# Attention in a two-layer hybrid decoder step: how far ahead of its use a unit's scores and sigmoid are made

## The chip, the cores and the metric

The kernel runs on one core of a Trainium2 chip. The metric is the device time of one execution of the whole program in microseconds (us), lower is better. Engines are named as the profile names them: PE is TensorE (matmuls and transposes; PEld are its weight loads), DVE is VectorE, ACT is ScalarE, POOL is GpSimd, SP is SyncE. Each engine works through its own instructions in the order in which they were written, and the engines hand work to each other through semaphores.

## The reference

Two layers (`DEPTH = 2`), each on a prompt of 1024 rows and on 8 sample sequences of 8 rows with a paged past of 4096. A layer projects the normed input into three token mixers side by side: retention (6 heads), stick-breaking attention (5 heads, "sb") and forgetting attention (5 heads, "fox"); their gated outputs are joined, projected, and a per-layer embedding is added. All is float32. What matters here are the two attentions on the prompt:

```python
# stick-breaking, a block of 128 query rows pb
z = einsum('bthd,bshd->bhts', qb, k) * scale
mask = k_pos < pb
ln1m = where(mask, log_sigmoid(-z), 0)
excl = reverse cumulative sum of ln1m, without the own element
a = where(mask, exp(log_sigmoid(z) + excl), 0)
out = einsum('bhts,bshd->bthd', a, v)

# forgetting
s = einsum(...) * scale + c_query - c_key
p = softmax(where(k_pos <= pb, s, -inf))
out = einsum('bhts,bshd->bthd', p, v)
```

## The kernel before, in words

A layer goes through phases that all engines leave together: projections and retention, then sb attention on the prompt (`ATT_S`), sb decoding of the samples, projections, fox attention on the prompt (`ATT_F`), fox decoding, output projections. The change lies in the two attention phases. With two layers each runs twice, so there are four such stages in the program.

An attention stage is a list of 40 **units**, `UNITS` at L466: 8 blocks of 128 query rows, the longest first (`t` from 7 down to 0, `i = 7 - t`), and in each block 5 heads (`h` from 0 to 4). A unit has `n = (t + 1) * 128` keys: 1024 in the first block, 128 in the last. I call the five units of a block a row of units, by its n. The steps of a unit u, with the engine and the line:

- **scores** (PE, L946): queries times keys into PSUM banks 0 and 1 or 2 and 3, by the parity of u.
- For sb: **sigmoid** (ACT, `first`, L1404) from PSUM into `sig[:, u % 2]`. Then **stick** (DVE, L1856, L1857, L1860, L1864): mask the diagonal block, take one minus it, scan the product backwards, multiply. It writes `att[:, u % 2]` and counts `att_probs`.
- For fox: **largest** (DVE, L1872 and L1875): mask the diagonal block in PSUM and take the row maximum. Then **exp** (ACT, `first`, L1413) from PSUM into `expd[:, u % 2]` with the sum of the row.
- **turn** (PE, L958): `t + 1` transposes of the weights into PSUM banks 4 and 5, which have no second copy. It waits for the stick (sb) or the exp (fox) of u and for the copy of unit u-1.
- **copy** of the turned weights (ACT, `to_sbuf`, L1424) to one of three SBUF buffers.
- **weigh** (PE, L972): turned weights times values. It is issued for a pair of heads after h = 1 and h = 3 and for the last head alone after h = 4.
- Once a row of units: **copy out** (ACT, `copy_out`, L1431 and L1432), **back** (PE, L984, three transposes), **finish** (DVE, L1887; in fox also L1884 and L1886), which gates the result into `O`. They belong to the row before and are issued while the next row is under way: copy out after h = 1, back at h = 2, finish after h = 3.

Nothing plans the order: it is the order in which the loops are written out. On PE the turn of u stands behind the scores of u+1, the weigh of u-1 and, at h = 2, the back. On ACT the copy of u stands behind the sigmoid or exp of u+1. On DVE it is stick or largest by unit, with finish behind the unit with h = 3.

Two waits bound how far ahead a step can go: scores of u wait until the sigmoid or exp of u-2 has read the PSUM banks (`att_first`, L943), and the sigmoid of u waits until the stick of u-2 is through with `sig` (`att_probs`, L1403). The exp of u waits for the turn of u-2.

Of the kernel before, what the change touches and what calls it, by code (L numbers as in the profile page):

```python
# [214 lines left out]
def step_program(nc, x_prompt, x_sample, state_ret, cache_sb_k, cache_sb_v, cache_fox_k,  # L215
# [10 lines left out]
    with ExitStack() as ctx:  # L226
# [220 lines left out]
        def phase_over(eng, n):  # L447

            eng.drain().then_inc(phase_sem, 1)  # L449
            eng.wait_ge(phase_sem, 4 * (n + 1))  # L450
# [15 lines left out]
        UNITS = [(t, NT - 1 - t, h) for t in reversed(range(NT)) for h in range(HA)]  # L466
# [9 lines left out]
        def weighed(u):  # L476

            t, i, h = UNITS[u]
            return QP * i + h // 2 + 1
# [6 lines left out]
        def bank2(first, n=1024):  # L486
            return ps[:, first:first + 2, :].rearrange("p b c -> p (b c)")[:, 0:n]
# [266 lines left out]
        def _(pe):  # L754
# [177 lines left out]
            def attention(phase):  # L932
                kind = KIND[phase]
                qT, kT, v = (qT_s, kT_s, v_s) if kind == "sb" else (qT_f, kT_f, v_f)

                def scores(u):
                    t, i, h = UNITS[u]
                    n = (t + 1) * P
                    q = slice((h % 2) * HD, (h % 2) * HD + HD) if kind == "sb" else slice(0, HD + 1)
                    a = h // 2 if kind == "sb" else h  # L940
                    if u >= 2:

                        pe.wait_ge(att_first[kind], u - 1)  # L943
                    for c in range(0, n, 512):
                        w = min(512, n - c)
                        ins = pe.matmul(ps[:, 2 * (u % 2) + c // 512, 0:w], qT[q, a, t * P:(t + 1) * P],  # L946
                                        kT[q, a, c:c + w], start=True, stop=True)
                    ins.then_inc(att_scores[kind], 1)

                def turn(u):  # L950
                    t, i, h = UNITS[u]

                    pe.wait_ge(att_probs[kind] if kind == "sb" else att_first[kind], u + 1)
                    if u >= 1:
                        pe.wait_ge(attT_ready[kind], u)
                    src = att if kind == "sb" else expd
                    for j in range(t + 1):
                        ins = pe.transpose(ps[:, 4 + j // 4, (j % 4) * P:(j % 4 + 1) * P],  # L958
                                           src[:, u % 2, j * P:(j + 1) * P], ident)
                    ins.then_inc(att_turned[kind], 1)  # L960

                def weigh(u):

                    t, i, h = UNITS[u]
                    pe.wait_ge(attT_ready[kind], u + 1)
                    c = h // 2
                    if c == 0 and i >= 2:
                        pe.wait_ge(att_done[kind], i - 1)
                    heads = [(a, 2 * c + a) for a in range(2) if 2 * c + a < HA]
                    for j in range(t + 1):  # L970
                        for a, hh in heads:
                            ins = pe.matmul(ps[a * HD:(a + 1) * HD, 6 + t % 2, c * P:(c + 1) * P],  # L972
                                            v[:, j, hh * HD:(hh + 1) * HD],
                                            attT[kind][(u - h + hh) % 3][:, j * P:(j + 1) * P],
                                            start=(j == 0), stop=(j == t), tile_position=(0, a * HD),
                                            skip_group_check=True)
                    ins.then_inc(att_out[kind], 1)

                def back(t):

                    pe.wait_ge(att_copied[kind], NT - t)
                    for c in range(QP):
                        w = min(P, DA - c * P)
                        ins = pe.transpose(ps[:, 6 + t % 2, c * P:c * P + w], att_oT[kind][0:w, c * P:(c + 1) * P],  # L984
                                           ident[0:w, 0:w])
                    ins.then_inc(att_back[kind], 1)

                scores(0)
                for u, (t, i, h) in enumerate(UNITS):
                    if u + 1 < len(UNITS):  # L990
                        scores(u + 1)
                    if u >= 1 and UNITS[u - 1][2] in (1, 3, 4):
                        weigh(u - 1)
                    if h == 2 and i >= 1:
                        back(t + 1)
                    turn(u)
                weigh(len(UNITS) - 1)
                back(0)
                phase_over(pe, phase)
# [203 lines left out]
            with pe.Fori(0, DEPTH) as L:  # L1203
# [5 lines left out]
                project(PROJ_SEGS[PROJ_S], L)  # L1209
                phase_over(pe, PROJ_S)  # L1210
                attention(ATT_S)
                decode(DEC_S, L)
                project(PROJ_SEGS[PROJ_F], L)
                phase_over(pe, PROJ_F)
                attention(ATT_F)
                decode(DEC_F, L)
                turn_mixed(0)
# [19 lines left out]
        def _(act):  # L1237
# [155 lines left out]
            def attention(phase):  # L1393
                kind = KIND[phase]

                def first(u):
                    t, i, h = UNITS[u]
                    n = (t + 1) * P
                    if kind == "sb":
                        act.wait_ge(att_scores[kind], u + 1)  # L1400
                        if u >= 2:

                            act.wait_ge(att_probs[kind], u - 1)  # L1403
                        act.activation(sig[:, u % 2, 0:n], bank2(2 * (u % 2), n), ACT.Sigmoid)\  # L1404
                            .then_inc(att_first[kind], 1)
                    else:
                        act.wait_ge(att_max, u + 1)
                        if u >= 2:
                            act.wait_ge(att_turned[kind], u - 1)

                        if h == 0 and i >= 2:
                            act.wait_ge(att_done[kind], i - 1)
                        act.activation(expd[:, u % 2, 0:n], bank2(2 * (u % 2), n), ACT.Exp,  # L1413
                                       bias=small[:, 40 + u % 4:41 + u % 4],
                                       accum_out=small[:, 50 + (t % 2) * HA + h:51 + (t % 2) * HA + h])\
                            .then_inc(att_first[kind], 1)

                def to_sbuf(u):
                    t, i, h = UNITS[u]
                    act.wait_ge(att_turned[kind], u + 1)  # L1420
                    if u >= 3:
                        act.wait_ge(att_out[kind], weighed(u - 3))
                    n = (t + 1) * P
                    act.activation(attT[kind][u % 3][:, 0:n], bank2(4, n), ACT.Copy).then_inc(attT_ready[kind], 1)  # L1424

                def copy_out(t):

                    act.wait_ge(att_out[kind], QP * (NT - t))
                    if t < NT - 1:
                        act.wait_ge(att_back[kind], NT - 1 - t)  # L1430
                    act.activation(att_oT[kind][:, 0:2 * P], ps[:, 6 + t % 2, 0:2 * P], ACT.Copy)  # L1431
                    act.activation(att_oT[kind][0:HD, 2 * P:3 * P], ps[0:HD, 6 + t % 2, 2 * P:3 * P], ACT.Copy)\  # L1432
                        .then_inc(att_copied[kind], 1)

                first(0)
                for u, (t, i, h) in enumerate(UNITS):
                    if u + 1 < len(UNITS):
                        first(u + 1)
                    to_sbuf(u)
                    if h == 1 and i >= 1:  # L1440
                        copy_out(t + 1)
                copy_out(0)
                phase_over(act, phase)
# [707 lines left out]
```

## Time and profile before

| | us |
|---|---|
| median of 3 runs | 3688.18 |
| the 3 runs | 3682.5, 3688.18, 3698.48 |
| the profiled execution | 3678.38 |
| its span | 3676.8 |
| sb attention, layer 1 and layer 2 | about 460 to 598, 2288 to 2424 of the span |
| fox attention, layer 1 and layer 2 | about 1092 to 1224, 2915 to 3047 |

Over the span PE is busy 3204.2 us (87%), DVE 1365.4 (37%), ACT 950.5 (26%). The profile is one execution; a group of its instructions is named by line, engine, operation and output and input. "Idle before, releaser" is how long an engine stood still before an instruction and whose semaphore ended it. The granted clock (PEclk) is 1.00 when PE runs at 2.4 GHz and 0.50 at 1.2 GHz. Instructions of the same kind that follow each other are merged in a timeline, with their count behind an x; the duration of a merged PE row contains the tail of its last matmul, so the next row can start up to 0.2 us before it ends. A float32 score matmul of 512 columns shows as two records.

### The profile page before, as it was taken

How to read it: one execution, taken by the hardware profiler on the slowest of the kernel's cores; microseconds unless marked ns; L12 is line 12 of the kernel's file. 1: busy time of each engine (PE TensorE's matmuls, PEld its weight loads, DVE VectorE, ACT ScalarE, POOL GpSimd, SP SyncE). 2: the span in 40 equal slices, each digit the busy share in tenths (PEclk: the TensorE clock that was granted, in tenths of full speed). 3: DMA queues.
4: the chain of work that ended last, by engine and by line, in shares of the span. 5: the costliest groups of instructions: out<-in, count | busy, mean ns of one | idle time of the engine just before them, and what ended most of it. 6: DMA issues, size and time to landing. Idle time of an engine off the chain costs nothing. (4 is left out here: it accounts for less than half of the span.)

```text
span 3676.8 us, 67694 instructions
## 1 busy us (share of the span) xinstructions
PE 3204.2 (87%) x25256; PEld 1989.8 (54%) x25256; DVE 1365.4 (37%) x3002; ACT 950.5 (26%) x1746; POOL 597.8 (16%) x1090
## 2 busy tenths in 40 slices
PE   6999987888998688799989998978889987887998
PEld 4556654555666455444455666545556654554443
DVE  3235086443224444312142350954433244442211
ACT  2012144332224333211020122433322242331110
POOL 0000000444010044400000000004440101452000
PEclk9999988999999799899989999989999997998999
DMA  5011103887120388710120011048861205995102
GB/s 175 18 36 33 50 10 105 265 287 244 38 83 1 117 278 290 249 66 16 46 96 28 28 45 44 1 129 288 284 217 33 72 1 173 295 299 186 57 29 72
DMA packets 268657, 439.67 MB, mean 120 GB/s; under 512 B 48818, under 2 KB 216403, under 8 KB 268339
## 3 DMA queue, kind: packets, MB, share of 16 engines
q1 hardware_dynamic: 205810, 239.96, 20.4%
q0 software_dynamic: 55744, 189.25, 15.6%
q10 hardware_dynamic: 6912, 7.87, 0.6%
q8 instruction: 126, 2.06, 0.2%
q14 instruction: 65, 0.52, 0.0%
HBM read 410.28 MB, written 26.65 MB: 119 GB/s over the span
## 5 line engine op out<-in xcount | busy, mean ns | idle before, releaser
L806 PE MATMUL ps<-W,xT 128*128 128x320 f32 (+7 forms) x5120 | 1482.9, 465 | 11.5 <-DVEq L449 11.5
L806 PEld LDWEIGHTS ps<-W,xT 128*128 128x128 f32 (+1 forms) x5120 | 856.7, 184 | 585.6 <-issue 291.5
L688 POOL DMA_DIRECT2D branch<-in_cache_sb_v_dram x480 | 258.8, 539 | 637.5 <-issue 597.3
L688 POOL DMA_DIRECT2D branch<-in_cache_fox_v_dram x480 | 258.9, 539 | 621.2 <-issue 579.6
L1468 ACT ACTIVATE branch<-ps 128x512 f32<-128x512 f32 x288 | 165.6, 595 | 386.6 <-PE ps L1051 378.2
L1051 PE MATMUL ps<-C,W 128*128 128x128 f32 x1280 | 199.4, 301 | 73.1 <-DMA W<-in_cache_fox_k_dram 26.6
L1051 PE MATMUL ps<-C,branch 128*128 128x128 f32 x1280 | 194.9, 295 | 65.7 <-DMA branch<-in_cache_sb_k_dram 18.0
L1136 PE MATMUL ps<-branch 128*8 128x64 f32 x9920 | 182.2, 234 | 55.9 <-DMA branch<-in_cache_fox_v_dram 27.6
L1073 PE MATMUL ps<-branch,work 128*32 128x512 f32 x896 | 229.9, 631 | 0.8 <-issue 0.2
L1051 PEld LDWEIGHTS ps<-C,W 128*128 128x128 f32 x1280 | 151.0, 151 | 141.0 <-issue 67.4
L1051 PEld LDWEIGHTS ps<-C,branch 128*128 128x128 f32 x1280 | 147.8, 149 | 146.3 <-issue 96.1
L946 PE MATMUL ps<-branch 64*128 64x512 f32 (+7 forms) x480 | 209.4, 564 | 19.9 <-POOLq L449 19.9
L1136 PEld LDWEIGHTS ps<-branch 128*8 128x8 f32 x9920 | 158.8, 99 | 79.7 <-issue 33.9
L1980 DVE COPY branch<-ps 128x512 f32<-128x512 f32 x160 | 107.8, 688 | 199.8 <-PE ps L1051 199.6
L1476 ACT ACTIVATE work<-ps 128x512 f32<-128x512 f32 x160 | 92.2, 597 | 317.5 <-PE ps L1073 317.5
L652 POOL DMA_DIRECT2D out_dram<-work x32 | 17.7, 552 | 742.9 <-ACT work L1292 549.0
L1073 PE MATMUL ps<-W,work 128*32 128x512 f32 x384 | 136.0, 657 | 1.6 <-issue 1.6
L946 PEld LDWEIGHTS ps<-branch 64*128 64x128 f32 (+1 forms) x480 | 85.7, 210 | 81.3 <-issue 59.9
L1995 DVE COPY branch<-ps 128x64 f32<-128x64 f32 x256 | 46.3, 226 | 211.7 <-PE ps L1087 160.8
L1087 PE MATMUL ps<-C,work 128*128 128x128 f32 x640 | 102.6, 293 | 24.2 <-ACT work L1476 24.2
L1692 DVE TENSOR_TENSOR work<-ps,branch 128x512 f32<-128x512 f32 (+1 forms) x40 | 25.5, 638 | 251.0 <-PE ps L806 250.6
L1860 DVE TENSOR_TENSOR_SCAN branch<-branch 128x1024 f32<-128x1024 f32 (+7 forms) x80 | 108.7, 1358 | 2.7
(246 smaller groups left out, 3389.1 us busy)
## 6 DMA issues: line engine op xcount, KB each, us to landing
branch<-in_cache_sb_v_dram POOLq DMA_DIRECT2D x480, 160.0 KB, 4.3
branch<-in_cache_fox_v_dram POOLq DMA_DIRECT2D x480, 160.0 KB, 4.1
W<-in_cache_sb_k_dram SPq DMA_DIRECT2D x248, 160.0 KB, 3.4
W<-in_cache_fox_k_dram SPq DMA_DIRECT2D x248, 160.0 KB
branch<-in_cache_sb_k_dram SPq DMA_DIRECT2D x240, 160.0 KB, 4.2
branch<-in_cache_fox_k_dram SPq DMA_DIRECT2D x240, 160.0 KB, 4.3
W<-in_w_in_dram SPq DMA_DIRECT2D x14, 1280.0 KB, 6.3
W<-in_w_in_dram SPq DMA_DIRECT2D x9, 1536.0 KB, 7.1
```

The costliest lines, as they stand in the source:

```text
L688: pool.dma_start(ringV[:, g % 2, p * DA:(p + 1) * DA], cache[L, bass.ds(pg, 1)].rearrange("a s h d -> s (a h d)"))\
L806: ins = pe.matmul(out, src[:, k, t * P:t * P + R], W[i % 2][:, k, a:z], start=(k == 0), stop=(k == kc - 1), **place)
L946: ins = pe.matmul(ps[:, 2 * (u % 2) + c // 512, 0:w], qT[q, a, t * P:(t + 1) * P], kT[q, a, c:c + w], start=True, stop=True)
L1051: ins = pe.transpose(ps[:, n % 2, m * P:(m + 1) * P], ringK[g % 2][:, at:at + P], ident)
L1073: ins = pe.matmul(ps[q:q + 32, bank, :], q_now[:, kk, :], kT_d[(5 * g + kk) % SLOTS], start=True, stop=True, tile_position=(0, q), skip_gr ...
L1087: ins = pe.transpose(ps[:, 6 + j % 2, m * P:(m + 1) * P], z_rows[:, 2 if j == 4 else j % 2, m * P:(m + 1) * P], ident)
L1136: ins = pe.matmul(out(h, a), pr[:, h, :, g * PG8 + first + p], values[:, c:c + HD], start=False, stop=False, tile_position=(0, 32 * a), sk ...
L1468: act.activation(kT_d[n % SLOTS], ps[:, n % 2, :], ACT.Copy).then_inc(s["kt_act"], 1)
L1476: act.activation(z_rows[:, 2 if j == 4 else j % 2, :], ps[:, 3 if j == 4 else (5 if j % 2 else 2), :], ACT.Copy)\
L1860: link(dve.tensor_tensor_scan(prod[:, e:SEQ][:, ::-1], r[:, ::-1], r[:, ::-1], 1.0, ALU.mult, ALU.bypass))
L1980: dve.tensor_copy(kT_d[n % SLOTS], ps[:, n % 2, :]).then_inc(s["kt_dve"], 1)
L1995: dve.tensor_copy(by_pair[:, j, 2 * NEW * kk:2 * NEW * (kk + 1), :, 0], src[:, kk, 0:2 * NEW])
```

## The change

On PE the scores of the first two units are made ahead of the loop, and the loop then makes those of u+2 where it made those of u+1. On ACT, in the sb stages alone, the sigmoids of the first two units stand ahead of the loop, and the loop makes that of u+2 ahead of the copy of u. In the fox stages ACT keeps its order (`ahead = 1`), and DVE keeps its order in both. No semaphore, buffer, instruction or operand is added or removed; the waits inside each step are the same.

```diff
                 scores(0)
+                scores(1)
                 for u, (t, i, h) in enumerate(UNITS):
-                    if u + 1 < len(UNITS):
-                        scores(u + 1)
+                    if u + 2 < len(UNITS):
+                        scores(u + 2)
                     if u >= 1 and UNITS[u - 1][2] in (1, 3, 4):
                         weigh(u - 1)
                     if h == 2 and i >= 1:
...
                 first(0)
+                ahead = 2 if kind == "sb" else 1
+                if ahead == 2:
+                    first(1)
                 for u, (t, i, h) in enumerate(UNITS):
-                    if u + 1 < len(UNITS):
-                        first(u + 1)
+                    if u + ahead < len(UNITS):
+                        first(u + ahead)
                     to_sbuf(u)
                     if h == 1 and i >= 1:
                         copy_out(t + 1)
```

ACT, the first units of an sb stage, before (L1404 is the sigmoid, L1424 the copy of turned weights; semaphores that a row waits for stand in brackets):

```order
L1404 ACTIVATE branch<-ps 128x1024 [waits phase_sem]
L1404 ACTIVATE branch<-ps 128x1024 [waits att_scores_sb]
L1424 ACTIVATE work<-ps 128x1024 [waits att_turned_sb]
L1404 ACTIVATE branch<-ps 128x1024 [waits att_probs_sb,att_scores_sb]
L1424 ACTIVATE work<-ps 128x1024 [waits att_turned_sb]
```

And the same place after the change (the lines are numbered one higher there):

```order
L1405 ACTIVATE branch<-ps 128x1024 [waits phase_sem]
L1405 ACTIVATE branch<-ps 128x1024 [waits att_scores_sb]
L1405 ACTIVATE branch<-ps 128x1024 [waits att_probs_sb,att_scores_sb]
L1425 ACTIVATE work<-ps 128x1024 [waits att_turned_sb]
L1405 ACTIVATE branch<-ps 128x1024 [waits att_probs_sb,att_scores_sb]
```

The third sigmoid now stands ahead of the first copy, and so on down the stage: each sigmoid is one copy earlier.

PE, in a fox stage, from the back of the first row of units on (L984 back, L958 turn, L946 scores, L972 weigh), before:

```order
L984 MATMUL ps<-C,branch 128x64
L958 MATMUL ps<-C,work 128x128 [waits attT_ready_fox,att_first_fox]
L958 MATMUL ps<-C,work 128x128 x6
L946 MATMUL ps<-branch 128x512 [waits att_first_fox]
L946 MATMUL ps<-branch 128x384
L958 MATMUL ps<-C,work 128x128 [waits attT_ready_fox,att_first_fox]
L958 MATMUL ps<-C,work 128x128 x6
L946 MATMUL ps<-branch 128x512 [waits att_first_fox]
L946 MATMUL ps<-branch 128x256
L972 MATMUL ps<-work,branch 64x128 [waits attT_ready_fox]
```

And after:

```order
L984 MATMUL ps<-C,branch 128x64
L958 MATMUL ps<-C,work 128x128 [waits attT_ready_fox,att_first_fox]
L958 MATMUL ps<-C,work 128x128 x6
L946 MATMUL ps<-branch 128x512 [waits att_first_fox]
L946 MATMUL ps<-branch 128x256
L958 MATMUL ps<-C,work 128x128 [waits attT_ready_fox,att_first_fox]
L958 MATMUL ps<-C,work 128x128 x6
L946 MATMUL ps<-branch 128x512 [waits att_first_fox]
L946 MATMUL ps<-branch 128x256
L972 MATMUL ps<-work,branch 64x128 [waits attT_ready_fox]
```

The pattern of steps stays; what moved is which unit the scores belong to. Behind the back stood the scores of the last unit of this row (896 keys, 512 and 384); now the scores of the first unit of the next row stand there (768 keys, 512 and 256), and those of the last unit are already ahead of the back.

## Rows read from the trace of the kernel before

**Rows 1.** Stretches: us, busy us (instructions) of PE, PEld, DVE, ACT, POOL, PEclk

```profile
463.00:594.00 131.00, 111.73 (x674) 68.25 (x670) 115.23 (x167) 55.76 (x94) 0.00 (x0) 0.89 0.00 1
1097.00:1220.00 123.00, 103.52 (x674) 68.86 (x672) 53.31 (x110) 60.20 (x134) 0.00 (x0) 0.90 0.01 3
```

**Rows 2.** Waits of DVE, sb stages of layers 1 and 2: total us, times, longest

```profile
DVE branch L1856 <- ACT branch L1404: 14.1, 10, 5.8
...
DVE branch L1856 <- ACT branch L1404: 12.7, 8, 6.2
```

**Rows 3.** The same view, last row of units of the sb stage, layer 1

```profile
DVE branch L1856 <- ACT branch L1404: 1.8, 3, 0.8
```

**Rows 4.** Timeline of DVE, sb layer 1: where sticks 0, 4 and 5 start

```profile
466.12 0.29 DVE L1856 TENSOR_TENSOR branch<-branch,C 128x128 f32<-128x128 f32 x1 [5.82 <-ACT branch L1404]
...
490.36 0.29 DVE L1856 TENSOR_TENSOR branch<-branch,C 128x128 f32<-128x128 f32 x1 [2.60 <-ACT branch L1404]
...
494.88 0.28 DVE L1856 TENSOR_TENSOR branch<-branch,C 128x128 f32<-128x128 f32 x1
```

**Rows 5.** Timeline of ACT, same stage: the sigmoid of unit 4

```profile
489.30 1.03 ACT L1404 ACTIVATE branch<-ps 128x1024 f32<-128x1024 f32 x1 [0.89 <-PE ps L946]
```

**Rows 6.** Stretches of that stage where the clock rises and where it is low again

```profile
484.00:488.00 4.00, 4.00 (x26) 3.26 (x23) 3.69 (x3) 0.61 (x1) 0.00 (x0) 0.63 0.00 0
...
588.00:592.00 4.00, 4.00 (x15) 2.33 (x15) 2.88 (x10) 1.72 (x7) 0.00 (x0) 0.50 0.00 0
```

**Rows 7.** Waits of PE for the copy, fox stages of layers 1 and 2

```profile
PE ps L972 <- ACT work L1424: 11.9, 12, 1.4
PE ps L972 <- ACT branch L1424: 6.1, 5, 1.5
...
PE ps L972 <- ACT work L1424: 11.7, 12, 1.4
PE ps L972 <- ACT branch L1424: 5.9, 5, 1.4
```

**Rows 8.** The same view, last row of units of the fox stage, layer 1

```profile
PE ps L972 <- ACT branch L1424: 1.5, 1, 1.5
PE ps L972 <- ACT work L1424: 1.2, 3, 0.6
```

**Rows 9.** Timeline of PE, fox layer 1, row of units of 640 keys

```profile
1172.67 0.76 PE L958 MATMUL ps<-C,work 128*128 128x128 f32 x5
1173.27 1.25 PE L946 MATMUL ps<-branch 65*128 65x512 f32 x4
1174.36 0.71 PE L958 MATMUL ps<-C,work 128*128 128x128 f32 x5
1174.90 1.02 PE L946 MATMUL ps<-branch 65*128 65x512 f32 x2
```

**Rows 10.** Timeline of ACT and DVE at the same place

```profile
1173.47 0.70 ACT L1424 ACTIVATE branch<-ps 128x640 f32<-128x640 f32 x1 [1.47 <-PE ps L958]
...
1173.53 0.49 DVE L1887 TENSOR_TENSOR O<-O,ps 128x320 f32<-128x320 f32 x1
1174.56 0.30 DVE L1872 TENSOR_TENSOR ps<-ps,C 128x128 f32<-128x128 f32 x1 [0.54 <-PE ps L946]
1174.89 0.82 DVE L1875 TENSOR_REDUCE small<-ps 128x1 f32<-128x640 f32 x1
...
1175.75 0.79 ACT L1413 ACTIVATE work<-ps,small 128x640 f32<-128x640 f32 x1 [1.57 <-DVE small L1875]
```

**Rows 11.** Duration of the maximum and the exp over all shapes: ns min/median/max

```profile
L1875 DVE TENSOR_REDUCE small<-ps x80: 291/758/1226, 1096.4 to 3038.8; 128x1 f32<-128x1024 f32 x10, 128x1 f32<-128x896 f32 x10, 128x1 f32<-128x768 f32 x10, 128x1 f32<-128x640 f32 x10
...
L1413 ACT ACTIVATE work<-ps,small x80: 359/740/1117, 1099.0 to 3039.2; 128x1024 f32<-128x1024 f32 x10, 128x896 f32<-128x896 f32 x10, 128x768 f32<-128x768 f32 x10, 128x640 f32<-128x640 f32 x10
```

**Rows 12.** Stretches of the fox stages with the clock below full, layers 1 and 2

```profile
1116.00:1148.00 32.00, 27.99 (x184) 20.43 (x183) 12.09 (x22) 14.20 (x23) 0.00 (x0) 0.84 0.00 1
...
2940.00:2948.00 8.00, 6.96 (x52) 5.61 (x53) 1.85 (x3) 3.11 (x5) 0.00 (x0) 0.79 0.01 2
```

## The prediction

> **What bounds the kernel now.** I read the page first: 40 units run in each of four attention stages, some 540 us of the span of 3676.8 (the table of stages). Nothing outside these stages is touched, so a gain can only come from what engines stand still in them. Next came the busy time of the two kinds of stage: in sb DVE is busy 115.2 of 131 us and PE 111.7; in fox PE is busy 103.5 of 123 us, and DVE and ACT 53 and 60 [rows 1]. So sb goes by DVE and fox by PE, and the question is who makes that engine wait. The view of waits answers it. In sb DVE waits for the sigmoid (L1404), 14.1 us in layer 1 and 12.7 in layer 2, of which 5.8 and 6.2 are the very first one [rows 2]. In fox PE waits in front of the weigh for the copy (L1424), 18.0 and 17.6 us in 17 waits each [rows 7]. The timeline then shows what the awaited instruction itself had waited for.
>
> **sb, what moves.** Before, the scores of u+1 stood on PE in front of the turn of u, and on ACT the sigmoid of u+2 stood behind the copy of u, which needs that turn. Now both are one unit earlier. The sigmoid of u+2 needs only its scores and the end of the stick of u, and DVE is by then busy with the stick of u+1, so the sigmoid lies beside a whole stick. The copy gives way by one sigmoid (1.03 us at 1024 keys [rows 5]); it is waited for by the weigh, behind scores on an engine with slack. Nothing is issued more often, there is no DMA among the steps, and SP's and POOL's queues are not passed.
>
> The waits that can go are 14.1 - 5.8 = 8.3 and 12.7 - 6.2 = 6.5, 14.8 us [rows 2]; the first wait stays, since scores and sigmoid of unit 0 come as before. Two deductions. In the last row of units DVE waits 1.8 us [rows 3] while PE is busy all the time at the lower clock [rows 6], so there PE sets the pace and an earlier place in the order gives little: I take off 1.8 for each layer and give back 0.3 for each, for the gap before the last turn. And in the first row PE runs at the lower clock until late in the stretch of [rows 6], about 487. A stick of 1024 keys takes 494.88 - 490.36 = 4.52 us; four of them from 466.12 end at 484.2 and the fifth at 488.7, while sticks 4 and 5 began at 490.36 and 494.88 [rows 4]. If the clock rises no earlier, PE makes the scores of unit 5 where it made those of unit 4, just ahead of the sigmoid at 489.30 [rows 5], and stick 5 begins where stick 4 did, at 490.36: 4.5 us gained and 1.6 left as a wait. If PE, which now has the scores of unit 2 to do in its pause ahead of the first turn, gets its clock earlier, none is left. Between 0 and 1.6 in layer 1, and less in layer 2, whose waits are smaller, I take 0.9 together. sb: 14.8 - 3.6 + 0.6 - 0.9 = 10.9 us.
>
> **fox, what goes.** ACT's order is exp of u+1, then copy of u. Before, where no weigh stood between (after h = 1 and h = 3), PE ran scores of u+1, turn of u, scores of u+2, and then the weigh of u waited: the copy was behind the exp of u+1, that behind the maximum, and that behind scores just made. Now those scores were made a unit earlier, the exp of u+1 can run while PE turns u, and the copy is ready when the weigh comes. That takes away the 35.6 us [rows 7] except in the last row of units, where no scores are left to fill with and 2.7 us stay in each layer [rows 8]: 35.6 - 5.4 = 30.2.
>
> **fox, what comes.** The scores of u+2 now wait for the exp of u, one step closer than before. DVE keeps its order, and there the finish of the row before stands ahead of the maximum of the unit with h = 4. Before, that was covered, since DVE was through with the finish and still waited 0.54 us for scores [rows 10]. Now the scores are there and the finish is late: it waits for the back. At 640 keys: the finish ends at 1174.02, the mask takes 0.33, the maximum 0.82, hand-over 0.04, the exp 0.79 [rows 10], and I take 0.15 (an estimate) for the read of the row's sum and the semaphore: 1176.15. PE has behind the back only a turn (0.60 from start to start), the scores of the next row (512 keys, 1.02, of which 0.95 to the next start) and a turn (0.54) [rows 9], from 1172.67 to 1174.76. Then it waits 1.4 us at the scores. Queued behind them are the weigh of h = 3 and the turn of h = 4; ACT's copy of h = 3 is behind the same exp. With 128 keys fewer the chain shortens by 0.13 + 0.11 = 0.24 (from 128 to 1024 keys in seven steps [rows 11]), the two turns by 0.22 (0.54 for five blocks) and the scores by about 0.22 (1.25 to 1.02), so the wait grows by 0.2. From 896 to 256 keys: 1.0, 1.2, 1.4, 1.6, 1.8, 2.0, together 9.0 us. The row of 1024 has no finish, the last row no further scores. At h = 1 the loop turn, copy (0.70), exp (0.79), scores takes 0.25 more in hand-overs, 1.74, against 1.09 + 0.54 of PE's own work at 640 keys [rows 9, 10]: a wait of 0.1, up to 0.3 in short rows, 0.7 for a stage. New waits: 9.7 a layer, 19.4 in all. Net fox: 30.2 - 19.4 = 10.8 us. Its bounds: 0, if each new wait is as long as the two that it replaces, and 30.2, if none comes.
>
> **Clock.** In the long fox rows the clock falls for short stretches: 0.84 over 32 us and 0.79 over 8 us [rows 12]. At half speed that is 10.2 and 3.4 us of low clock, half of which, 6.8 us, is lost. I lay them to PE's waits, of up to 1.4 us [rows 7]. Half of the waits go, the others stay: I take 2.0 of the 6.8.
>
> The Trainium skill (TensorE: Matmul & The Clock Gate, "A second HAM failure mode: psum-queue depth-cycling") says that a PE which pauses briefly between groups of matmuls as it cycles through PSUM banks can have its clock swing between the two levels. The stretches of [rows 12] agree with it. By that rule the new wait, which stands exactly at a bank's reuse, would keep the swings, and the term of 2.0 would be 0.
>
> **Sum.** 10.9 + 10.8 + 2.0 = 23.7 us off the profiled execution, 3678.4 to 3654.7. The profiled execution is the lowest of four; their median (3678.38, 3682.5, 3688.18, 3698.48) is 3685.3, which I take as the level that runs have: 3685.3 - 23.7 = 3661.6, about 3661.
>
> **Rivals.** (1) *Only half of it comes.* The place of a wait moves but the fox stage stays as long, because the new waits at the scores are as long as the old at the weigh (each copy of h = 3 still hangs on the exp of h = 4). For it: one finish and one maximum are in the way in six of eight rows. Against: the row of 640 keys gives 1.4 against two waits of about 1.1. Or sb gains only its small waits, since the low clock in its first row is what makes the sigmoid late. Gain 10 to 15, time 3672.
> (2) *The clock helps.* PE has fewer pauses, so the swings of [rows 12] go entirely (6.8) and the low start of sb is shorter: gain 35, time 3650.
> (3) *The clock turns against it; slower.* The new wait at the scores of h = 4 comes in every row from 896 to 256 keys, also where the clock is now full. If each is followed by a low stretch, PE, which bounds fox, pays half of that stretch. From the stretches of [rows 12], 13.6 us in about four falls, a fall lasts 3.4 and costs 1.7; twelve of these cost 20 and only cancel the gain. To be slower by 0.5% (18.4 us) the low stretches must cover 2 x (18.4 + 23.7) = 84 us of the two fox stages' 246 [rows 1]. The time is then 3704. For it: four falls in the longest rows. Against: none in the short rows, whose waits are as frequent.
> (4) *It does not do what it says.* The order moves but the sigmoid still comes late, because its `att_probs` wait (stick of u) holds it. It then starts at the end of the stick of u, still one stick before it is needed (4.52 us at 1024 keys), so only the shortest rows could show it: time 3664 to 3675, counted with (1).
>
> **How the numbers follow.** Forecast 0.55, with its own range 3650 to 3670; (1) and (4) 0.27; (2) 0.13; (3) 0.05. About 0.5% (18.4 us) is what can be told from no change here. Faster by more than that: 0.55 x 0.9, all of (2), a sixth of (1), together 0.67. Within: 0.27. Slower: 0.06. The range of 8 in 10, 3640 to 3683, takes in (1) and (2), and the 10 us by which runs of one program differ.
>
> **What would show it.** sb: the waits of DVE for L1404's successor fall from 14.1 and 12.7 to about 7 to 8 each, nearly all of it the first wait. The sb stage shortens by 5 to 6 us from its first scores to its last finish. fox: PE's waits for the copy before the weigh fall to some 3 us, and a new line appears, scores waiting for the exp, of 8 to 11 us a layer in about six long waits, each after the finish. Each fox stage shortens by 5 to 7 us. The rest of the span does not move by more than 1 us a phase. The prediction is wrong if PE's waits in fox come to more than 15 us a layer, if the clock in the fox stages averages lower than 0.90, or if DVE still waits in sb rows of 768 keys and fewer.

## The result, and the profile after

The changed kernel takes 3661.15 us (median of 13 runs, 3648.96 to 3671.11), the kernel before 3683.21 us (13 runs, 3672.94 to 3698.48). The ratio is 0.9932, 95% interval 0.9915 to 0.9949: 0.7% or 25 us faster (19 to 31); the medians are 22 us apart. The forecast was about 3661. The total agrees, but one of its terms had the wrong sign, and much of what follows is about that term.

The profiled execution of the changed kernel took 3671.11 us, the highest of its 13, with a span of 3669.6. I therefore read the stages in it, not its total. Four stretches, each from the first scores of a stage on PE to the end of its last finish on DVE, in the order sb, fox, sb, fox. The columns are us, busy us (instructions) of PE, PEld, DVE, ACT, POOL, then PEclk, DMA share, GB/s. Before:

```profile
460.23:597.79 137.56, 116.65 (x684) 70.40 (x684) 115.84 (x169) 56.58 (x97) 0.00 (x0) 0.87 0.02 5
1092.19:1224.16 131.97, 110.21 (x684) 71.80 (x684) 55.36 (x114) 61.02 (x137) 2.02 (x2) 0.88 0.03 9
2288.01:2424.36 136.35, 115.00 (x684) 68.94 (x684) 115.93 (x169) 56.57 (x97) 0.00 (x0) 0.88 0.02 6
2915.26:3044.89 129.63, 108.63 (x684) 69.95 (x684) 55.37 (x114) 61.02 (x137) 2.02 (x2) 0.88 0.03 9
```

After:

```profile
462.08:593.29 131.21, 117.85 (x684) 70.74 (x684) 114.96 (x169) 56.77 (x97) 0.00 (x0) 0.86 0.02 6
1090.70:1221.33 130.63, 118.47 (x684) 74.95 (x684) 54.54 (x114) 60.13 (x137) 2.02 (x2) 0.81 0.03 9
2284.43:2415.87 131.44, 117.90 (x684) 70.63 (x684) 114.96 (x169) 56.77 (x97) 0.00 (x0) 0.86 0.02 7
2903.87:3031.62 127.75, 115.72 (x684) 73.08 (x684) 54.55 (x114) 60.13 (x137) 2.03 (x2) 0.83 0.03 9
```

The sb stages are 6.35 and 4.91 us shorter, 11.3 together. The fox stages are only 1.34 and 1.88 shorter, 3.2 together. Read a fox row as "length minus PE busy": PE stands still 21.8 us before and 12.2 after in layer 1, 21.0 and 12.0 in layer 2. So 9.6 and 9.0 us of standing still are gone, more than forecast. But the same 684 matmuls now take 8.3 and 7.1 us longer, because the granted clock fell from 0.88 to 0.81 and 0.83. Outside these four stages the profiled execution is 7.3 us longer, in code that is unchanged. That belongs to the single execution (the second profile of the same program, below, does not show it).

DVE's waits in the two sb stages (total us, times, longest), to be held against [rows 2]. The lines of after are numbered a little higher: L1404 is L1405, L1413 is L1414, L1424 is L1425, L1856 is L1860, L1887 is L1891.

```profile
DVE branch L1860 <- ACT branch L1405: 7.3, 3, 5.8
DVE O L1891 <- PE ps L984: 4.7, 2, 3.7
...
DVE branch L1860 <- ACT branch L1405: 7.6, 3, 6.0
```

14.1 and 12.7 fell to 7.3 and 7.6, of which 5.8 and 6.0 are the first wait. The second line is a cost that I did not have. The finish in sb waits for the back 4.7 us, where it was 3.2 before. DVE now comes to it earlier, and the back does not. DVE's timeline against [rows 4] shows the wait that is left:

```profile
467.99 0.29 DVE L1860 TENSOR_TENSOR branch<-branch,C 128x128 f32<-128x128 f32 x1 [5.85 <-ACT branch L1405]
...
486.06 0.28 DVE L1860 TENSOR_TENSOR branch<-branch,C 128x128 f32<-128x128 f32 x1
491.93 0.29 DVE L1860 TENSOR_TENSOR branch<-branch,C 128x128 f32<-128x128 f32 x1 [1.26 <-ACT branch L1405]
```

Five sticks run back to back, and the sixth waits 1.26 us. The clock, 0.64 from 486 to 490 and 1.00 for some 85 us from then on, rises no earlier after the stage's start than before, which was the slower of the two cases in the prediction (1.6 us left). The wait left in layer 2 is 1.35 us.

PE's waits in the fox stage of layer 1, against [rows 7]:

```profile
PE ps L946 <- ACT work L1414: 7.1, 7, 1.3
...
PE ps L972 <- ACT branch L1425: 1.2, 1, 1.2
...
PE ps L972 <- ACT work L1425: 0.4, 1, 0.4
```

Layer 2 has the same values. The 18 us ahead of the weigh are 1.6, and the new line, scores waiting for the exp, has 7.1 us in 7 waits. The place in the row of 640 keys, to be held against [rows 9, 10], DVE and ACT first, then PE:

```profile
1164.71 0.49 DVE L1891 TENSOR_TENSOR O<-O,ps 128x320 f32<-128x320 f32 x1
1165.11 0.29 DVE L1876 TENSOR_TENSOR ps<-ps,C 128x128 f32<-128x128 f32 x1
1165.44 0.82 DVE L1879 TENSOR_REDUCE small<-ps 128x1 f32<-128x640 f32 x1
...
1166.30 0.80 ACT L1414 ACTIVATE work<-ps,small 128x640 f32<-128x640 f32 x1 [0.94 <-DVE small L1879]
...
1167.24 1.21 PE L946 MATMUL ps<-branch 65*128 65x512 f32 x2 [1.00 <-ACT work L1414]
```

The chain is the one forecast, link by link: finish, mask, maximum, exp, scores. Its wait is 1.00 us instead of 1.4. The first and the last of the six such waits of the stage (the seventh of the 7.1 us is one of 0.88 in the first row, where PE waited 0.9 before too):

```profile
1135.49 1.56 PE L946 MATMUL ps<-branch 65*128 65x512 f32 x4 [0.83 <-ACT work L1414]
...
1206.23 0.80 PE L946 MATMUL ps<-branch 65*128 65x128 f32 x2 [1.25 <-ACT work L1414]
```

The six are 0.83, 0.92, 1.00, 1.08, 1.17 and 1.25, together 6.25 us. They grow by 0.08 a row, not by 0.2. Last, the clock in the same stage. Stretches of after, the first in the long rows, the others in the short ones:

```profile
1110.00:1166.00 56.00, 54.23 (x414) 38.01 (x412) 27.24 (x51) 30.41 (x55) 0.00 (x0) 1.00 0.00 1
1166.00:1174.00 8.00, 7.00 (x43) 4.66 (x41) 3.14 (x7) 3.52 (x8) 0.00 (x0) 0.79 0.00 0
...
1206.00:1214.00 8.00, 7.69 (x32) 5.00 (x32) 2.08 (x8) 3.21 (x16) 0.00 (x0) 0.50 0.00 1
1148.00:1216.00 68.00, 60.10 (x354) 38.66 (x350) 30.75 (x75) 31.35 (x89) 0.00 (x0) 0.82 0.00 1
```

And the last of these stretches in the kernel before, at the same distance from the stage's start to within 2 us, with PE's waits for the copy in it:

```profile
1148.00:1216.00 68.00, 55.11 (x401) 36.47 (x399) 32.81 (x75) 35.62 (x94) 0.00 (x0) 1.00 0.00 1
```

```profile
PE ps L972 <- ACT work L1424: 8.9, 9, 1.4
PE ps L972 <- ACT branch L1424: 3.3, 3, 1.2
```

The two kernels have exchanged places. Before, the clock fell in the long rows [rows 12] and was full in the short ones; now it is full in the long rows and falls to its lower level (1.2 GHz) in the short ones, first around the wait of 1.00 us that ends at 1167.24. Behind the two shorter ones it had stayed full. The length of a wait alone does not decide this: before, PE stood still twelve times in these 68 us, 12.2 us in all and up to 1.4 at a time, and the clock stayed at 1.00. A small part of the 8.3 and 7.1 us comes earlier: the low clock at the start of a fox stage lasts some 19 us after its first scores, where it was 16, about 1.5 us of loss at half speed (an estimate from slices of 4 us). That is so in e4 and e8 too.

### The profile page after: what moved, and what is told of

It reads as the page before. It is cut to its first block and busy times, and to the rows that moved or that the text cites. A ratio compares the mean times of both kernels' runs of the same rounds, so it can differ in the third digit from the quotient of the medians.

```text
span 3669.6 us, 67694 instructions
## 1 busy us (share of the span) xinstructions
PE 3224.6 (88%) x25256; PEld 1995.1 (54%) x25256; DVE 1362.0 (37%) x3002; ACT 949.2 (26%) x1746; POOL 597.8 (16%) x1090
## 5 line engine op out<-in xcount | busy, mean ns | idle before, releaser
L946 PE MATMUL ps<-branch 64*128 64x512 f32 (+7 forms) x480 | 222.8, 594 | 38.9 <-POOLq L449 19.8
L1052 PE MATMUL ps<-C,branch 128*128 128x128 f32 x1280 | 191.2, 291 | 59.1 <-DMA branch<-in_cache_sb_k_dram 15.4
L946 PEld LDWEIGHTS ps<-branch 64*128 64x128 f32 (+1 forms) x480 | 89.2, 219 | 112.1 <-issue 56.4
```

The costliest lines, as they stand in the source:

```text
L1052: ins = pe.transpose(ps[:, n % 2, m * P:(m + 1) * P], ringK[g % 2][:, at:at + P], ident)
```

## The experiments

**One half at a time.** Kernel e1 keeps the change in sb alone, e2 in fox alone, and e3 is the changed kernel once more, beside them.

```
-                scores(1)
+                far = 2 if kind == "sb" else 1      # e2: "fox", and ahead = 1 on ACT
+                if far == 2:
+                    scores(1)
...
-                    if u + 2 < len(UNITS):
-                        scores(u + 2)
+                    if u + far < len(UNITS):
+                        scores(u + far)
```

Expected of e1:

> Scores two units ahead and the sigmoid two ahead in the sb stages alone; the fox stages are as before. Theory (both parts gain; sb by letting the sigmoid lie beside a stick): each sb stage 5 to 6 us shorter than before, 131 us instead of 137, DVE's waits for the sigmoid 7 to 8 us with the first one, the whole 10 to 12 us faster (ratio 0.997). The fox stages 130 to 132 us as before, PE's waits there 18 us for the copy. Rival (all of the gain is fox): ratio 1.000.

Expected of e2:

> Scores two units ahead in the fox stages alone; the sb stages are as before. Theory: PE's waits in a fox stage fall from 18 us for the copy to 7 us for the exp and about 2 for the copy. By the waits alone each stage would be 9 us shorter; the changed kernel's profile shows 1.3 and 1.9 us, with the granted clock down from 0.87 to 0.81 and from 0.88 to 0.83. If the clock's low stretches in the short rows vary from run to run, the whole is 3 to 18 us faster and the runs spread wider than those of before. Rival (the clock always takes the gain): whole within 4 us of before.

Expected of e3:

> The changed kernel once more, for a second profile beside the others on one chip. Theory (the parts add): its gain is the sum of those of the sb part and the fox part, 20 to 24 us (ratio 0.9935). Theory of the clock: the times of its profiled executions go with the granted clock of the fox stages; where the stages show 0.87 or more they take 122 to 125 us, where they show 0.81 they take 130. Rival: the stages take 130 us whatever the clock, and the profiled execution was long elsewhere.

Measured (before 3682.99): e1 3665.74 us, ratio 0.9968 (0.9939 to 0.9996). e2 3679.66 us, ratio 0.9984 (0.9964 to 1.0005). e3 3659.8 us, ratio 0.9948 (0.9928 to 0.9967). So sb brings about 12 us by the ratio and 17 by the medians, and fox alone 6 and 3, which its interval does not tell from nothing, nor the theory of e2 from its rival; its runs (3654 to 3688) don't spread wider than those of before (3656 to 3698), as I had thought they might. In e1's profile the fox stages take 129.8 and 132.0 us, as expected, and the sb stages 131.3 and 128.7, the second 2.3 below what I expected. The two ratios add to that of e3 (0.32% and 0.16% against 0.52%). The fox stages of e2, then of e3:

```profile
1094.45:1223.37 128.92, 116.74 (x684) 73.56 (x684) 54.54 (x114) 60.06 (x137) 2.02 (x2) 0.83 0.03 9
2913.91:3044.52 130.61, 118.46 (x684) 74.94 (x684) 54.53 (x114) 60.05 (x137) 2.02 (x2) 0.81 0.03 9
```

```profile
1087.67:1221.28 133.61, 122.42 (x684) 77.36 (x684) 54.52 (x114) 60.06 (x137) 2.01 (x2) 0.78 0.03 9
2904.01:3032.04 128.03, 115.16 (x684) 72.81 (x684) 54.54 (x114) 60.06 (x137) 2.02 (x2) 0.85 0.03 9
```

The low clock comes with this order of fox in all six stages profiled (two each of the changed kernel, e2 and e3), by varying amounts from 0.78 to 0.85, and the stage's length goes roughly with it, from 133.6 us at 0.78 to about 128 at 0.83 and 0.85. No stage of this order reached 0.87, so that part of e3's theory stays untried. In e3 all that lies outside the four stages takes 3141.4 us, before 3141.3: the change reaches nothing else.

**Take the new wait away.** In e4 the finish of the row before stands behind the maximum of the unit with h = 4, in fox alone:

```
-                    if h == 3 and i >= 1:
+                    if h == (4 if kind == "fox" else 3) and i >= 1:
                         finish(t + 1)
```

> The changed kernel with one more edit: in the fox stages DVE does the finish of the row before after the maximum of h = 4 instead of ahead of it. Theory (the new wait at the scores comes from the finish in front of that maximum): PE's waits for the exp fall from 7 us in 7 waits to under 2 us a stage, and if pauses bring the clock down, its low stretches in the rows of 512 to 256 keys go too; 3 to 12 us faster than the changed kernel. Rival (the exp itself is too late, by ACT's order of copy and exp): the 7 us stay.

Measured: 3625.33 us (3621.84 to 3636.82, 6 runs), ratio to before 0.986 (0.9829 to 0.989). The two fox stages, and PE's waits in the first:

```profile
1076.51:1190.65 114.14, 108.56 (x684) 68.43 (x684) 55.35 (x114) 60.18 (x137) 2.01 (x2) 0.90 0.04 10
2872.21:2986.21 114.00, 108.42 (x684) 68.31 (x684) 55.36 (x114) 60.18 (x137) 2.02 (x2) 0.90 0.04 10
```

```profile
PE ps L946 <- ACT work L1414: 0.9, 1, 0.9
...
PE ps L972 <- ACT work L1425: 0.6, 2, 0.4
```

The six waits are gone; only the one in the first row is left. A fox stage falls from 130.6 and 127.8 to 114 us. The waits were 6.25 us a stage, and 16.5 and 13.8 came: PE is busy 9.9 and 7.3 us less as well, since the clock stays up. This is the fastest kernel of the study, about 35 us below the changed one, where I had expected 3 to 12. Fox gives 30 of these 35; the other 5 are the sb stages, which are 2.6 and 2.7 us shorter with an unchanged order (see e9 below).

**Price the clock by itself.** e8 leaves the wait where it is, but gives PE ten small transposes to do in it, whose result nobody reads. Everything else is the changed kernel.

```
+                def fill(t, n):
+                    for _ in range(n):
+                        pe.transpose(ps[:, 6 + t % 2, 3 * P:4 * P], ident, ident)
...
+                    if kind == "fox" and h == 4 and i >= 1:
+                        fill(t, 10)
                     if u + 2 < len(UNITS):
                         scores(u + 2)
```

> The changed kernel with ten more transposes (of the identity, into PSUM columns that nothing reads) on PE in the fox stages, at h = 4 from the second row on, right where PE waits for the exp ahead of its scores. The waiting stays, PE is just not idle in it. Theory (two thirds of the cost of these waits is that PE's clock falls after them in the short rows): the granted clock of the fox stages rises from 0.78 to 0.85 to 0.88 or more, and a stage takes 120 to 124 us instead of 128 to 134, though PE does 7 us more work. Rival (the clock falls for another reason, such as the lighter work of the short rows): clock as in the changed kernel, stage 130 to 136 us.

Measured: 3649.87 us (4 runs; before 3682.66 beside it), ratio 0.990 (0.987 to 0.993).

```profile
1084.12:1205.42 121.30, 115.47 (x754) 75.83 (x754) 54.54 (x114) 60.13 (x137) 2.01 (x2) 0.92 0.04 10
2893.20:3014.51 121.31, 115.48 (x754) 75.84 (x754) 54.54 (x114) 60.13 (x137) 2.02 (x2) 0.92 0.03 9
```

The scores still can't start before the exp, but PE waits only 1.0 us for it in the whole stage. It has 70 more instructions (ten in each of seven rows of units); yet the stage is 6.4 to 9.3 us shorter than in the changed kernel and the clock is 0.92. Against e4 it is 7.2 us longer, which is about the waits themselves. So of the 16.5 and 13.8 us between the changed kernel and e4, 9.3 and 6.4 are clock and 7.2 are wait. In this order it is PE standing still at the scores that costs the clock: filled or removed, the clock is 0.92 or 0.90. It is no rule for every pause, since the kernel before kept 1.00 over twelve waits of up to 1.4 us.

**Is it the finish alone?** e7 has e4's edit, but fox's scores one unit ahead as before.

> sb as in the changed kernel; in fox the scores are one unit ahead as before, and the finish stands behind the maximum of h = 4. It tells whether the 16 us by which that edit shortens a fox stage of the changed kernel come of the edit itself or of both together. Theory (before, the finish was covered, DVE waited for scores anyway): fox stages 129 to 132 us as before, PE's waits for the copy 17 to 18 us. Rival (the finish was late in the kernel before as well): fox stages under 125 us.

Measured: 3666.56 us, ratio 0.9955 (0.993 to 0.9979), which is e1 within the intervals.

```profile
1083.56:1215.76 132.20, 110.56 (x684) 71.91 (x684) 54.71 (x114) 61.26 (x137) 2.01 (x2) 0.87 0.03 9
2896.06:3030.48 134.42, 113.79 (x684) 74.08 (x684) 54.70 (x114) 61.38 (x137) 2.00 (x2) 0.84 0.03 9
```

Without the earlier scores the waits of [rows 7] stay (11.6 and 6.5 us in layer 1), and moving the finish brings nothing; layer 2 is even 2.4 us above the expected range, at a clock of 0.84. With them it brings the 16.5 and 13.8 us of e4. Neither edit is worth much alone in fox.

**The two parts of sb.** e5 has the scores of sb early and the sigmoid as before; e6 the sigmoid early and the scores as before (fox as before in both).

```
e5:  far = 2 in sb;  ahead = 1 on ACT
e6:  far = 1;        ahead = 2 on ACT in sb
```

> Only the scores go two units ahead, in the sb stages alone; ACT keeps its old order (sigmoid of u+1, copy of u) and fox is as before. Theory (in the first row the sigmoid waited for scores made at the lower clock, so the scores' place is what counts): most of the sb gain is there, a stage of 131 to 133 us against 137.5 before and 131.3 with both. Rival (ACT's order is what counts): the stage stays at 136 to 137.

> Only the sigmoid goes two units ahead on ACT in the sb stages; the scores stay one unit ahead on PE, in sb and fox. Theory: the sigmoid of u+2 then stands ahead of the copy of u and waits for scores that PE makes only after the turn of u, so DVE's waits stay (12 to 14 us a stage) and the copy comes later: stage 137 to 142 us, whole no faster than before. Rival (ACT's order is what counts): stage 131 to 133 us.

Measured: e5 3676.62 us, ratio 0.9979 (0.9962 to 0.9997); its sb stages take 133.8 and 132.8 us, between those of before and after. DVE waits for the sigmoid 11.3 us in 4 waits and 10.3 in 3. The early scores alone give 3.8 and 3.6 of the stages' 6.3 and 4.9 us, the early sigmoid on top the rest; layer 1 lies just outside the range that I gave for e5. e6 is where I was wrong by far: 3844.53 us, ratio 1.0431 (1.0398 to 1.0463). The sb stage of layer 1 takes 228.3 us where I had expected about 140. Its first 134 us, the rest, and a place in its row of 768 keys:

```profile
456.84:591.00 134.16, 97.00 (x431) 62.77 (x432) 73.89 (x79) 32.32 (x43) 0.00 (x0) 0.64 0.02 6
591.00:685.00 94.00, 72.11 (x254) 38.98 (x254) 44.60 (x90) 20.23 (x54) 0.00 (x0) 0.52 0.00 1
```

```profile
548.98 0.81 ACT L1407 ACTIVATE branch<-ps 128x768 f32<-128x768 f32 x1 [5.70 <-PE ps L946]
549.68 0.81 ACT L1427 ACTIVATE work<-ps 128x768 f32<-128x768 f32 x1
549.82 0.29 DVE L1862 TENSOR_TENSOR branch<-branch,C 128x128 f32<-128x128 f32 x1 [3.65 <-ACT branch L1407]
...
550.63 1.51 PE L958 MATMUL ps<-C,branch 128*128 128x128 f32 x6 [1.69 <-ACT work L1427]
```

ACT stands 5.70 us at the sigmoid of u+2, for scores that PE makes only late; the copy of u is queued behind it and starts at 549.68, though its turn is long done, and PE waits 1.69 us for that copy before it can go on. So PE waits for ACT and ACT for PE, once a unit, and the clock sinks to its lower level, at 0.52 over the last 94 us. The sigmoid may only go two ahead because the scores do.

**Two attempts at the rest of sb.** e9 is e4 with such transposes also in sb, ahead of the scores of unit 2 (20) and of the first two turns (20 and 12), to bring the clock up before the first stick. e10 is e4 with the later finish in sb too (`if h == 4 and i >= 1:` for both).

> The changed kernel with the finish behind the maximum of h = 4 in fox (as e4_finish_later), and in the sb stages idle PE at the very start filled with transposes that nothing reads: 20 ahead of the scores of unit 2, 20 ahead of the first turn, 12 ahead of the second. Theory (the wait of 1.3 us that the changed kernel keeps at unit 5 is owed to the lower clock of the first 25 us of the stage, which follows on PE's pauses there): the clock is full earlier, that wait is gone, an sb stage takes 127 to 130 us instead of 131.3, and the whole is 1 to 5 us faster than with the finish alone (3625). Rival (the clock of the start does not depend on these pauses): stage 131 us, wait unchanged.

> As e4_finish_later, and in the sb stages too the finish goes behind the stick of h = 4. In sb DVE waits 1.0 us for the back once, in the last row, and is otherwise never held up by the finish. Theory (DVE's waits in sb are the first sigmoid and little else): sb stages the same within 1.5 us, whole within 3 us of 3625. Rival (the finish holds sb back as it did fox): sb stages 3 us shorter or more.

Measured: e9 3631.5 us (3626.57 to 3637.19, 5 runs), ratio to its before 0.9874 (0.985 to 0.9899), no better than e4. The clock is 0.92 and 0.97 and the wait of 1.26 us is gone, but the sb stages are 129.2 and 128.1 us against e4's 128.6 and 128.7: DVE bounds them. e4 gets there by itself, with the same order in sb as the changed kernel: its stages of 128.7 have neither the 1.26 nor the additional 1.5 us at the finish, 2.7 together of the 131.3 in others. The same order of sb runs at about 131.3 or 128.7 from one program or layer to the next; in e4 the clock has risen some 25 us after the first scores, in the changed kernel some 27. The whole was not 1 to 5 us faster than e4, as I had expected of e9.

e10: 3649.61 us (before 3677.0 beside it), ratio 0.9927 (0.99 to 0.9954): 24 us slower than e4, which neither the theory nor the rival had. Its fox stages take 114 us as in e4; the two sb stages make 16 of the 24, and the rest of the profiled difference lies outside the four stages. Its sb stage in full and two stretches of it, then the same stretches of e4:

```profile
455.81:592.45 136.64, 126.26 (x684) 75.41 (x684) 115.38 (x169) 56.76 (x97) 0.00 (x0) 0.79 0.02 6
544.00:560.00 16.00, 14.18 (x85) 7.54 (x85) 15.35 (x27) 7.98 (x17) 0.00 (x0) 0.97 0.01 2
560.00:592.00 32.00, 30.10 (x116) 16.88 (x112) 20.06 (x53) 9.97 (x30) 0.00 (x0) 0.50 0.00 1
```

```profile
544.00:560.00 16.00, 13.76 (x85) 7.70 (x84) 15.31 (x28) 7.75 (x16) 0.00 (x0) 1.00 0.01 2
560.00:592.00 32.00, 22.29 (x132) 13.06 (x131) 25.05 (x70) 12.00 (x34) 3.79 (x7) 0.83 0.15 46
```

From the wait of 0.80 us for a stick at 558 on the clock is at its lower level to the end, PE becomes the bound (30.1 of 32 us busy), and the stage is 8 us longer. PE's waits for DVE up to 558 are fewer and shorter in sum than in e4 (4.6 us in 5 against 6.7 in 9), but after the slow start of the stage two of them are longer than any of e4's there (0.66):

```profile
530.39 0.77 PE L958 MATMUL ps<-C,branch 128*128 128x128 f32 x5 [1.05 <-DVE branch L1868]
...
558.14 0.55 PE L958 MATMUL ps<-C,branch 128*128 128x128 f32 x3 [0.80 <-DVE branch L1868]
```

The clock falls just behind these two and nowhere else between 490 and 560. Layer 2 shows the same pair. Even so, this gives no threshold: in the kernel before PE waits 1.14 us for a stick at 495 and four times 0.7 to 0.9 after it, and the clock is 1.00 from 490 to 580. What sets it apart isn't settled.

## Why the prediction was right, and where it was not

**sb: right.** Forecast 10.9 us, measured 11.3 in the pair of profiles and 11.8 (1.5 to 22.5) by e1's ratio. Step by step: waits of DVE for the sigmoid forecast at 7 to 8, found 7.3 and 7.6; left in the first row 0 to 1.6, found 1.26, with the mechanism given (the clock rises no earlier). But two terms were off and cancelled: 0.9 us was taken for both layers together, and 1.26 and 1.35 were left; in return DVE is busy 0.9 us less in each stage. In the last row of units 1.5 a layer was kept as a wait because PE sets the pace there. That size came out, but at another place: the waits for the sigmoid fell to 0.24 and 0.19, and the finish now waits 1.5 us more for the back.

**fox, what goes: right.** Forecast 35.6 - 5.4 = 30.2 us. Found: 35.6 less the 1.6 a layer that are left, 32.4.

**fox, what comes: right mechanism, size too big.** Forecast 9.7 a layer in about six long waits behind the finish; found 7.1. Against the 9.0 of the six long waits stand 6.25: the row of 640 keys gives 1.00 instead of 1.4, and the step from row to row is 0.08 instead of 0.2. The chain was nearly right, 3.39 us from the turn behind the back to the scores against a forecast of 3.48. PE's own work in it was put too low: 2.39 us against 2.09, since the scores take 1.05 to the next start instead of 0.95, and the second turn's record ends 0.74 after its start where 0.54 was taken. From row to row those scores shrink by 0.11, not by 0.22, which gives the step of 0.08 instead of 0.2. The new wait stands for two of 1.13 and 1.35 us in that row, not for two "of about 1.1", so rival (1) was further off than it looked. Against the 0.7 of the loop at h = 1 stands nothing; the remaining 0.88 is the wait at the stage's first exp, which only moved to another line. By the waits alone fox gained 9.3 a layer, 18.6 in all by standing still, where the forecast said 10.8.

**Clock: wrong in sign.** This is the step that failed: "Half of the waits go, the others stay: I take 2.0 of the 6.8." Found: 8.3 and 7.1 us more of busy PE, a loss of 15.4. I had taken the clock's fall as proportional to the sum of waits. What happened is rival (3) in the place that it named, the short rows, with about 15 us, near the 20 that its twelve falls would cost but far from the 42 that it needed to make the kernel slower. The point against it, "none in the short rows, whose waits are as frequent", read the trace rightly and concluded too much: twelve waits at the weigh left the clock full there, and the few new ones at the scores did not. e8 and e4 show by two ways of removing them that these waits cost the clock. Why they do and the old ones did not stays open. The Trainium skill (TensorE: Matmul & The Clock Gate, "A second HAM failure mode: psum-queue depth-cycling") would have had the swings go on, the term at 0 and not at 2.0; that was nearer, and the trace goes further in the same direction, 0.88 to 0.81. But the 68 us of before at a clock of 1.00 with twelve short waits show that such pauses need not bring the swings.

**The sum.** Forecast 23.7 = 10.9 + 10.8 + 2.0. Found in the stages 14.5 = 11.3 + 18.6 - 15.4, and 11.2 in e3's; by the medians 22.1, 25 (19 to 31) by their ratio, and 19 (12 to 27) by e3's. So the forecast came out partly by luck: the fox waits (18.6 for 10.8) and the clock (-15.4 for 2.0) were off in opposite directions. Runs of one program differ by 10 us and more, and the profiled executions of the changed kernel and of e3 were among their slowest, so the stages in them may show less than the median gains; the runs place the true gain only between some 12 and 31 us. Of the marks set beforehand, the fox clock below 0.90 and "each fox stage -5 to -7" were missed, and by the first the prediction calls itself wrong; it was badly set, as the clock was 0.88 over the whole stage before. "The rest of the span does not move" was missed in the one profile (7.3 us) and met in e3's (0.1).

## What to carry to other kernels

Before work is brought forward by a unit, look at what stands in front of the next link of the chain on its engine: here one small step (the finish, with no one waiting for it) ahead of a maximum cost most of the gain, and moving it behind gave more than the whole change. When PE gets a new wait, ask for its price twice, once as idle time and once for the clock, which can also be nothing, and read the clock from the trace after the change. Where the wait can't be removed, see whether harmless work can fill it. If an engine's step moves ahead, the step that feeds it has to move as far: the sigmoid moved without its scores was much worse than no change, while the scores moved alone did gain.

## What the runs showed of the hardware

- With six waits of 0.83 to 1.25 us at the scores a fox stage ran at a granted clock of 0.81 and 0.83. With ten small transposes in each of these places it was 0.92, and the stage 9.3 and 6.4 us shorter (e8); without the waits it was 0.90 (e4).
- Waits of the same length need not do this: before, PE stood still twelve times for up to 1.4 us between 1148 and 1216 of the span, and the clock was 1.00. What tells the two apart is open.
- An order in which PE and ACT wait for each other once a unit held the clock at its lower level for most of the stage: 228 us instead of 137, with PE busy only 169 (e6).
- With the same instructions in the same order the average clock of a stage still varies, even between the two layers of one execution (0.78 and 0.85 in the fox stages of e3), and with it the stage by 5.6 us.
- In sb a later finish brought the clock down some 20 us earlier, though PE paused less in sum; each of the two falls came behind a wait of 0.8 us or more (e10).
